# Attention woven between query units and its output projection, pooled units first in the first mixer, own tensors for the conv mixer's output parts

## The reference, cut to what matters

```python
def mixer_ab(x, w_in, ln_g, ln_b, w_s, b_s, pool_w, pool_scale, w_out):
    proj = x @ w_in                                   # 1024 -> 1536
    uv = jax.nn.gelu(proj[..., :2 * A_WIDTH])         # u, v: 512 each
    u, v = uv[..., :A_WIDTH], uv[..., A_WIDTH:]
    v = layer_norm(v, ln_g, ln_b)
    sp = jnp.einsum('gij,bnjgc->bnigc', w_m, vb) + b_s   # over blocks of 128 tokens
    y_a = u * sp.reshape(bsz, seq, A_WIDTH)
    xb = proj[..., 2 * A_WIDTH:]                      # 4 groups of 128
    pooled = [trailing_mean_minus_self(xb[:, :, g], w) for g, w in enumerate((2, 4, 8, 16))]
    y_b = einsum('bsgc,gcd->bsgd', pooled, pool_w) * pool_scale
    return jnp.concatenate([y_a, y_b], axis=-1) @ w_out

def mixer_c(x, w_in, conv_w, w_out):
    gate_b, gate_c, h = jnp.split(x @ w_in, 3, axis=-1)
    return (gate_b * causal_dwconv(gate_c * h, conv_w)) @ w_out

def cross_attend(x, mem, wq, wkv, wo):                # 4 heads of 256
    q = x @ wq
    k, v = mem @ wkv
    probs = jax.nn.softmax(q @ k.T * 256 ** -0.5)     # per head
    return (probs @ v) @ wo
```

## Time and profile before

| | us |
|---|---|
| median of 3 runs (2519.91 to 2522.45) | 2520.11 |
| the profiled execution's own time | 2517.44 |
| its span in the trace | 2515.7 |
| PE busy in it | 2442.0 (97%) |
| DVE busy | 1115.9 (44%) |
| ACT busy | 798.6 (32%) |
| POOL busy | 62.2 (2%) |
| mean granted TensorE clock | 0.985 of full |

### The profile page before, as it was taken

The page is one execution under the profiler, slowest core; times in us unless marked ns, Lnnn a source line. Parts: engine busy times, 40 slices in busy tenths (PEclk is TensorE's granted clock), DMA queues, the critical chain, the costliest instruction groups (busy, mean ns, idle before and its releaser), DMA issues.

```text
span 2515.7 us, 27187 instructions
## 1 busy us (share of the span) xinstructions
PE 2442.0 (97%) x12244; PEld 2051.2 (82%) x12244; DVE 1115.9 (44%) x1054; ACT 798.6 (32%) x871; POOL 62.2 (2%) x38
## 2 busy tenths in 40 slices
PE   9999999998999999998998999999999998999998
PEld 8888889976788888886986888888887976888886
DVE  4333236436753333236724644423534635544424
ACT  4222225433442222132333333322322432433311
POOL 0000000004100000001000000000001000000000
PEclk9999999998999999998999999999999999999999
DMA  4222313220122222241430322231332511222321
GB/s 156 101 96 88 117 67 118 85 76 1 67 84 101 99 87 108 84 156 51 168 117 0 115 87 100 101 114 70 125 110 84 184 67 37 103 96 101 114 89 65
DMA packets 34405, 238.30 MB, mean 95 GB/s; under 512 B 3949, under 2 KB 4333, under 8 KB 6514
## 3 DMA queue, kind: packets, MB, share of 16 engines
q1 hardware_dynamic: 34288, 236.56, 26.2%
q10 hardware_dynamic: 2, 0.00, 0.0%
HBM read 234.46 MB, written 2.10 MB: 94 GB/s over the span
## 4 chain that ended last, share of the span: by engine, by line
PE 93%; DVE 5%; ACT 1%; issue 1%; DMA 0%; POOL 0%; DVEq 0%; POOLq 0%; ACTq 0%
PE bank L419 50%; PE bank L493 27%; PE bank L458 4%; PE bank L767 4%; PE bank L481 1%; DVE w_lo L1278 1%; PE bank L803 1%; PE bank L693 1%; PE bank L780 1%; PE bank L726 1%; DMA raw<-w_full 0%; PE bank L648 0%; PE bank L653 0%; PE bank L639 0%; DVE pool L1661 0%
## 5 line engine op out<-in xcount | busy, mean ns | idle before, releaser
L419 PE MATMUL bank<-a_hi,w_hi 128*128 128x512 f32 (+1 forms) x2080 | 771.6, 371 | 4.4 <-DVE w_lo L1278 3.7
L419 PE MATMUL bank<-a_hi,w_lo 128*128 128x512 f32 (+1 forms) x2080 | 769.2, 370 | 0.0
L419 PE MATMUL bank<-a_lo,w_hi 128*128 128x512 f32 (+1 forms) x2080 | 769.1, 370 | 0.0
L1278 DVE TENSOR_TENSOR w_lo<-raw,w_hi 128x2048 fp32r<-128x2048 f32 x207 | 479.3, 2318 | 558.0 <-ACT w_hi L911 542.5
L911 ACT ACTIVATE w_hi<-raw 128x2048 fp32r<-128x2048 f32 x207 | 394.1, 1906 | 372.3 <-DMA raw<-w_full 372.3
L419 PEld LDWEIGHTS bank<-a_hi,w_hi 128*128 128x128 f32 x2080 | 392.5, 189 | 73.0 <-issue 3.8
L419 PEld LDWEIGHTS bank<-a_hi,w_lo 128*128 128x128 f32 x2080 | 392.4, 189 | 66.7 <-issue 0.5
L419 PEld LDWEIGHTS bank<-a_lo,w_hi 128*128 128x128 f32 x2080 | 392.3, 189 | 66.3
L493 PE MATMUL bank<-w_hi,h_hi 128*128 128x512 f32 x704 | 278.9, 396 | 0.0
L493 PE MATMUL bank<-w_hi,h_lo 128*128 128x512 f32 x704 | 278.4, 395 | 0.0
L493 PE MATMUL bank<-w_lo,h_hi 128*128 128x512 f32 x704 | 278.3, 395 | 0.0
(11 more groups left out here) (271 smaller groups left out, 2240.4 us busy)
## 6 DMA issues: line engine op xcount, KB each, us to landing
raw<-w_full SPq DMA_DIRECT2D x207, 1024.0 KB, 4.8
rows_ab<-rows SPq DMA_DIRECT2D x8, 1024.0 KB, 5.9
x<-x SPq DMA_DIRECT2D x4, 512.0 KB, 6.3
mem_raw<-mem SPq DMA_DIRECT2D x2, 1024.0 KB, 7.6
out<-x SPq DMA_DIRECT2D x4, 512.0 KB, 2.6
raw<-w_full SPq DMA_DIRECT2D x2, 512.0 KB, 6.3
ab_rows<-ab_rows SPq DMA_DIRECT2D x1, 768.0 KB, 6.3
wg_raw<-w_gates SPq DMA_DIRECT2D x1, 512.0 KB, 5.6
```

The source lines that it names most:

```text
L419: last = mm(bank[:, b + m, cols], w[:, s, c0:c0 + P], act_in[:, k, cols], start=(k == 0 and j == 0), stop=(k == KD - 1 and j == 2))
L1278: V.tensor_tensor(w_lo[:, u % SLOTS, :], raw[:, u % SLOTS, :], w_hi[:, u % SLOTS, :], ALU.subtract).then_inc(w_split, 1)
```

## The change

Four edits.

1. First mixer: the weights' order on the host becomes pool inputs, v, u. PE computes the pool inputs in units 0 and 1 with `head_units` (feature tiles over halves of the tokens), v in units 2 and 3 with `token_units`, u in 4 and 5, and `ab_pool` stands after unit 5 directly ahead of `ab_spatial`, which now waits for one group's pool output at a time. DVE does the trailing sums first and the normalisation behind them.
2. Conv mixer: `cout` reads tensors of its own, `y_hi` and `y_lo`, and each pair of rows is split as soon as its unit of `cin` is done.
3. Attention: PE's list weaves query tiles, scores, transposes, values and parts of `wo`. The queries use banks 0 and 1 alone, scores and values of a head share banks 2, 3 or 4, 5, transposes use 6, 7. The output's parts get own tensors, `o_hi` and `o_lo`.
4. Behind the attention: the parts are ordered so that slots of `wo` come free earlier (`out_used` before the last eight groups of matmuls), and `ln_out` splits the next phase's first unit and takes the first two token groups before it normalises the third.

The core of the diff (lines of context and the removed lines of the attention are left out):

```diff
+        y_hi = arena("y_hi", [P, KD, T], f32r, 24)
+        y_lo = arena("y_lo", [P, KD, T], f32r, 40)
...
+        o_hi = arena("o_hi", [P, KD, T], f32r, 48)
+        o_lo = arena("o_lo", [P, KD, T], f32r, 64)
...
-                return (SIG["sgu_v"], SIG["pool_in"], SIG["sgu_u"])[u // 2], u % 2 + 1
+                return (SIG["pool_in"], SIG["sgu_v"], SIG["sgu_u"])[u // 2], u % 2 + 1
...
-                    return rows_part(name, u, t, (a_hi, a_lo), k_of, u == 0, u == 3)
+                    acts = (y_hi, y_lo) if name == "cout" else (a_hi, a_lo)
+                    return rows_part(name, u, t, acts, k_of, u == 0, u == 3)
...
+                qn, wn = f"q{layer}", f"wo{layer}"
+                a0 = 4 * layer
+
+                def queries(u, m):
+                    if m == 0:
+                        pe.wait_ge(w_split, U0[qn] + u + 1)
+                    if u:
+                        pe.wait_ge(SIG["attn_q"], 8 * layer + 2 * u - 1 + m)
+                    elif m == 0:
+                        pe.wait_ge(*freed(f"kv{layer}", 6))
+                    feature_tile(qn, u, m, slice(0, T), 0).then_inc(gemm_done, 1)
+
+                def scores_of(h):
+                    b = 2 + 2 * (h % 2)
+                    pe.wait_ge(SIG["attn_q"], 8 * layer + 2 * h + 2)
+                    if h == 0:
+                        pe.wait_ge(*freed(f"kv{layer}", 7))
+                    elif h >= 2:
+                        pe.wait_ge(SIG["attn_o32"], a0 + h - 1)
                     for t in range(NT):
                         for d in range(2):
                             last = mm(bank[:, b + t // 2, (t % 2) * MEM:(t % 2) * MEM + MEM],
                                       q_at[:, 2 * h + d, t * P:(t + 1) * P], k_mem[:, 2 * h + d, :],
                                       start=(d == 0), stop=(d == 1))
                     last.then_inc(SIG["attn_scores_mm"], 1)
+
+                def probs_turn(h):
+                    pe.wait_ge(SIG["attn_probs"], a0 + h + 1)
+                    if h:
+                        pe.wait_ge(SIG["probs_t"], a0 + h)
                     for m in range(2):
                         for t in range(NT):
+                            last = nc.tensor.transpose(bank[:, 6 + m, t * P:(t + 1) * P],
+                                                       pe_at[:, h % 2, t, m * P:(m + 1) * P], ident[:, :])
                     last.then_inc(SIG["probs_transposed"], 1)
+
+                def values_of(h):
+                    b = 2 + 2 * (h % 2)
+                    pe.wait_ge(SIG["probs_t"], a0 + h + 1)
                     for d in range(2):
                         for m in range(2):
+                            last = mm(bank[:, b + d, :], v_mem[:, m, (2 * h + d) * P:(2 * h + d + 1) * P],
+                                      p_t[:, h % 2, m, :], start=(m == 0), stop=(m == 1))
                     last.then_inc(SIG["attn_out_mm"], 1)
+
+                def part(u, t):
+                    if t == 0:
+                        pe.wait_ge(w_split, U0[wn] + u + 1)
+                        pe.wait_ge(a_hi_k, hi_at(wn, 2 * u + 1))
+                        pe.wait_ge(*low_at(wn, 2 * u))
+                        pe.wait_ge(*low_at(wn, 2 * u + 1))
+                    if u == 0 and t == 0:
+                        pe.wait_ge(SIG["attn_q"], 8 * layer + 8)
+                    elif u == 0 and t < 3:
+                        pe.wait_ge(SIG["attn_o32"], a0 + 2 + t)
+                    return rows_part(wn, u, t, (o_hi, o_lo), lambda u: 2 * u, u == 0, u == 3)
+
+                queries(0, 0)
+                queries(0, 1)
+                queries(1, 0)
+                scores_of(0)
+                queries(1, 1)
+                queries(2, 0)
+                scores_of(1)
+                probs_turn(0)
+                queries(2, 1)
+                values_of(0)
+                queries(3, 0)
+                scores_of(2)
+                probs_turn(1)
+                queries(3, 1)
+                values_of(1)
+                part(0, 0)
+                scores_of(3)
+                probs_turn(2)
+                part(1, 0)
+                values_of(2)
+                probs_turn(3)
+                part(0, 1)
+                values_of(3)
+                part(1, 1)
+                part(2, 0)
+                part(2, 1)
+                part(3, 0).then_inc(y_done, 1)
+                part(3, 1).then_inc(y_done, 1)
+                part(0, 2)
+                part(0, 3).then_inc(out_used, 1)
+                part(1, 2)
+                part(2, 2)
+                turn(wn, 0)
+                turn(wn, 1)
+                part(3, 2).then_inc(y_done, 1)
+                part(1, 3).then_inc(out_used, 1)
+                part(2, 3).then_inc(out_used, 1)
+                part(3, 3).then_inc(y_done, 1)
...
-                pe.wait_ge(SIG["ab_yb"], 4)
                 for g in range(4):
+                    pe.wait_ge(SIG["ab_yb"], g + 1)
...
-            pe.wait_ge(a_lo_tok, TURN0["down1"] + 2)
-            for u in range(2):
-                pe.wait_ge(w_split, U0["ab"] + u + 1)
-                token_tile("ab", u, 0)
-                if u:
-                    turn("down1", 3)
-                token_tile("ab", u, 1)
-                if not u:
-                    turn("down1", 2)
-            for t in (2, 3):
-                pe.wait_ge(a_lo_tok, TURN0["down1"] + t + 1)
-                for u in range(2):
-                    last = token_tile("ab", u, t)
-                    if t == 3:
-                        last.then_inc(gemm_done, 2)
-            feature_units("ab", 2, 5)
+            head_units("ab", "down1")
+            token_units("ab", 2, 4)
+            feature_units("ab", 4, 6)
             ab_pool()
-            feature_units("ab", 5, 6)
...
+            split_upto(ab + 3)
+            for u in (0, 1):
                 act.wait_ge(gemm_done, gemm_at("ab", u))
-                S.activation(gv[:, :, u * 256:(u + 1) * 256],
-                             bank[:, 2 * u:2 * u + 2, :].rearrange("p b (t c) -> p (b t) c", t=2),
-                             ACT.Gelu_apprx_tanh).then_inc(SIG["sgu_v"], 1)
+                S.activation(pool[0][:, 2 * u:2 * u + 2, PAD:PAD + T], bank[:, 2 * u:2 * u + 2, :],
+                             ACT.Copy).then_inc(SIG["pool_in"], 1)
             for u in (2, 3):
                 split_upto(ab + u + 2)
+                b = 2 * (u % 2)
                 act.wait_ge(gemm_done, gemm_at("ab", u))
-                S.activation(pool[0][:, 2 * (u - 2):2 * (u - 2) + 2, PAD:PAD + T],
-                             bank[:, 2 * (u % 2):2 * (u % 2) + 2, :], ACT.Copy).then_inc(SIG["pool_in"], 1)
-                if u == 2:
-                    act.wait_ge(SIG["sgu_stats"], 4)
-                    S.activation(rs4[:, :], mv4[:, :, 1], ACT.Sqrt, bias=eps5).then_inc(SIG["sgu_std"], 1)
+                S.activation(gv[:, :, (u - 2) * 256:(u - 1) * 256],
+                             bank[:, b:b + 2, :].rearrange("p b (t c) -> p (b t) c", t=2),
+                             ACT.Gelu_apprx_tanh).then_inc(SIG["sgu_v"], 1)
+            act.wait_ge(SIG["sgu_stats"], 4)
+            S.activation(rs4[:, :], mv4[:, :, 1], ACT.Sqrt, bias=eps5).then_inc(SIG["sgu_std"], 1)
+            split_upto(ab + 6)
...
-                    act.wait_ge(SIG["c_y"], 4)
-                    for k in range(KD):
-                        S.activation(a_hi[:, k, :], yc[:, k, :], ACT.Copy).then_inc(a_hi_k, 1)
+                        if u >= 8:
+                            act.wait_ge(SIG["c_y"], u - 7)
+                            for k in (2 * u - 16, 2 * u - 15):
+                                S.activation(y_hi[:, k, :], yc[:, k, :], ACT.Copy).then_inc(a_hi_k, 1)
...
+                def out_high(g):
                     act.wait_ge(SIG["attn_o32"], 4 * layer + g + 1)
                     for d in range(2):
-                        S.activation(a_hi[:, 2 * g + d, :], o32[:, d, :], ACT.Copy).then_inc(a_hi_k, 1)
+                        S.activation(o_hi[:, 2 * g + d, :], o32[:, d, :], ACT.Copy).then_inc(a_hi_k, 1)
+                queries_out(0, 0)
+                split_upto(q0 + 2)
+                queries_out(0, 1)
+                queries_out(1, 0)
+                split_upto(q0 + 3)
+                exps(0)
+                queries_out(1, 1)
+                queries_out(2, 0)
+                split_upto(w0)
+                transposed(0)
+                exps(1)
+                queries_out(2, 1)
+                split_upto(w0 + 1)
+                out_high(0)
+                queries_out(3, 0)
+                transposed(1)
+                exps(2)
+                queries_out(3, 1)
+                split_upto(w0 + 2)
+                out_high(1)
+                transposed(2)
+                exps(3)
+                split_upto(w0 + 3)
+                transposed(3)
+                out_high(2)
+                out_high(3)
...
+                if name[0] == "w":
+                    split_upto(end)
```

(30 more changed lines are left out.)

201 lines of the change are left out of this document (67 added, 134 removed).

## The result

The changed kernel takes 2475.41 us (median of 4 runs, 2471.86 to 2476.40) against 2520.01 for the kernel before in the same comparison (4 runs, 2517.25 to 2522.45): a ratio of 0.982, 95% interval 0.9808 to 0.9832. It is faster by 44.6 us, beyond the 5 us that can be told from no change. The forecast of 2471 is 4.4 us low and the range of 2465 to 2481 holds the time. The profiled execution took 2474.66 us, with a span of 2472.9: 42.8 less than the span of the earlier trace rows.

The account below looks back on a forecast made before the run. PE's work bounds the kernel (93% of the chain), so only its waits and lower clock can be gained: 12.2 + 5.5 + 16.6 + 14.6 = 48.9, less half a microsecond 48.4, giving 2471 us, range 2465 to 2481.

Parts of the forecast that it names:

- First mixer: From the start of `ab` to the start of `about`: 88.85 us becomes 76.6, gain 12.2, bounds 10.5 to 12.5.
- Conv mixer: From the last product of `yc` to the end of `cout`: 49.3 us becomes 43.8, gain 5.5, bounds 3.9 and 5.5.
- Attention: From first query matmul to matmuls behind the last transpose: 148.3 and 146.3 us become 131.7, gains 16.6 and 14.6.
- four spots: First mixer, conv mixer and the attention in two layers, where PE waits or runs at the lower clock: gains sum to 48.9.
- main case: The forecast itself, chance 0.77: a time from 2465 to 2476 us.
- the walk: Attention: PE's, DVE's and ACT's lists followed, giving 130.3 us of work plus one wait of 1.4.
- Half a microsecond for handovers: Taken off the summed gain of 48.9 us for handovers between small groups, giving 48.4.
- The tail: Behind the attention: the first `wo` slot is free 18 us before the projection ends; next unit's load and split over at 112.4.
- DVE's list was not late: Rival, chance 0.14: in the weave DVE's list is late, costing 4.5 us a layer, time 2480.
- The clock did not oscillate in the weave: Rival, chance 0.04: five handovers in each layer's weave cost 1.7 us each by clock, 17 in all, time 2488.
- The weave hid what it was to hide: Rival, chance 0.03: the weave hides nothing, heads' chains wait as before, only the mixers gain, 17.7 us, time 2502.
- the kernel wasn't slower: Rival, chance 0.02: slower than before, the clock staying at its lower level through both weaves, up to 2735.

Follow-up runs that it names:

- e2: Kernel before with only the pool products moved behind unit 5, order of units and DVE's list unchanged: 2509.52 us, ratio 0.9955.
- e3: Kernel before with only the conv mixer's edit (`y_hi` and `y_lo` for `cout`, split in pairs): 2514.70 us, one run.
- e1: Changed kernel with the whole arena (the region of tensors from `A0` on) 64 bytes lower, at 128 above a multiple of 256: 2459.44 us, ratio 0.976.
- e4: Kernel before, not woven, with own tensors `o_hi` and `o_lo` for the attention's output: 2524.61 us, one run.
- e12: Kernel before with only the attention's tail changed (order of the last eight parts, and `ln_out`), heads not woven: 2513.41 us, one run.
- e6: Changed kernel with PE's old order of the attention's tail put back, DVE's and ACT's lists staying as changed: 2496.38 us, one run.
- e7: e1 with `cc` to `y_lo` 128 bytes lower (to 0) and the memory's three tensors 64 bytes lower (to 64): 2457.70 us, ratio 0.9758.
- e9: e7 with head 2's copy ahead of the last `wo` split, and `cc` to `y_lo` another 128 bytes lower: 2458.51 us, ratio 0.9756.
- e10: Changed kernel with the whole arena 192 bytes lower, at a multiple of 256 bytes: 2471.92 us, one run.

## Why the prediction was right, step by step

The mechanism was right in all four spots. The forecast was 4.4 us low, the time lies just under the 2476 that bounds its main case, and two terms of the sum carry most of that: the 43.8 of `cout` and the 2.72 of a part.

- **What bounds the kernel**: right. All gains came from the four spots, and PE's list is now filled: the wait for `o32` is the only one left in an attention.
- **First mixer**: 12.1 against 12.2. No pool product waits, DVE's list behind v fits as worked out, and the clock never falls. e2 shows what the order of the units is for.
- **Conv mixer**: 4.5 against 5.5. The start was right, the term "takes 43.8", taken from `about`, was mis-sized: it is 44.80, since `y_hi` and `y_lo` lie elsewhere than `a_hi` (shown by e3, and by moving the arena in e1). The separate tensors were on the list of edits costed at nothing.
- **Attention**: 15.2 and 13.2 against 16.6 and 14.6, so the prediction had 1.4 too much in each. The difference of 2.0 between the layers is no merit of the walk, which is one for both; it lies in the rows of before. The walk's ends of PE's pieces were predicted at 19.8, 34.2, 43.9, 52.8 and 62.6 us and lie at 19.80, 34.17, 43.94, 52.87 and 62.64 (1279.09, 1293.46 and so on, less 1259.29). Up to there PE doesn't wait, so this confirms that nothing was late, and beyond that it is a sum of known durations. The one wait, 1.4 in the walk, is 1.1, at the place named. What was mis-sized is the term "16 parts of 2.72": a part takes 2.80 (11.21 for four), 1.3 us in all, and this too is place, as e4 shows.
- **Half a microsecond for handovers**: the part of the shortfall that it was meant for is some 0.4 in the first attention: the part behind the wait takes 3.06 instead of 2.80, and the query tiles 43.66 in pieces instead of 43.56. With 1.3 for the parts and 0.3 less of wait that is the 1.4.
- **The tail**: right in its mechanism: the next phase's first unit is loaded and split under the projection, and PE has no wait behind it. It is worth 2.2 and 1.2 alone (e12). The 9.6 and 10.0 of e6 are mostly the price of one list put back without the others.
- **Rivals**: DVE's list was not late; every pass it owed came before it was wanted but one. The price beside POOL fell elsewhere than the prediction had it: the splits of `wo` units 1 and 2 took 2.28 us, and DVE's low parts beside POOL's 1.78 and 1.76 in place of 0.69; the maximum behind them wasn't late. The clock did not oscillate in the weave, 1.00 throughout, so the rule of the Trainium skill ("TensorE: Matmul & The Clock Gate", section "A second HAM failure mode: psum-queue depth-cycling") did not decide here, where the idle time between groups is at most 1.1 us. It fell behind waits of 1.2 and 3.0 us in e2. The weave hid what it was to hide, and the kernel wasn't slower.
- **The range**: its upper end follows from the terms. The lower end, 2465, doesn't: all terms at their best sum to 49.2, which is 2471 from the median, and 2468 without the wait of 1.4 in both layers. The time lay at the other end, so this did not decide.
- The remaining 2 us between the four spots (45.0) and the spans (42.8) are the unchanged part ahead of the first mixer, whose length differs from execution to execution; what decides its clock each time stays open.

Open as well: whether the slow place is one of the tensor itself or relative to the weights, which were never moved; whether the weave without the tail, in all lists, gives what the estimate says; and why the keys' and values' 256-column products take 21.77, 22.61, 22.78 or 23.03 us, once with no edit to the tensors that they read. Places of these tensors other than those named were not tried.

The fastest version here is the changed kernel with the arena at 128: e1 and its variants e7 to e9 have medians of 2457.4 to 2459.4 us, 0.7% under the changed kernel and 2.4% under the one before, and can't be told apart.

## What to carry to other kernels

Where one engine's work is the bound, walk the lists of all engines once over the new order with durations from the trace: the walk gave five ends of PE's work within 0.1 us, the one wait that was left at its place, and its length within 0.3. A matmul's duration belongs to the tensors that it reads as well as to its shape, so a change that gives an operand a new tensor has to be priced with that, and the place of each hot operand is worth a run of its own. An order that frees slots early lies in the lists of several engines at once: put back on PE alone it cost 9.6 and 10.0 us, where the whole of it, measured in the kernel before, brought 2.2 and 1.2. To learn what such an edit is worth, take it out of all lists.

## What the runs showed of the hardware

A matmul of 128x512 in fp32r takes 226.7, 232.4 or 233.4 ns by where its 128x128 operand (or the tensor around it) lies within 256 bytes (e1, e10, the changed kernel), 2.5 to 3% in 528 matmuls in a row. Over the program the place of the arena was worth 16 us (e1), more than a third of what the whole change brought. The 256-column products do not follow the same rule: they are slowest (23.03 for 192) where the wide ones are fastest, and in e7 they took 22.61 and 21.77 at one and the same place. A split on DVE took 3.29 us in place of 2.29 in e2, where POOL makes low parts during the first third of it, about 1 us more as in the earlier trace rows; in the changed kernel a low part of 128x512 beside POOL's took 1.78 in place of 0.69. That POOL is the cause was not tested by a run of its own.
